# One fp32 decoder layer on one core: expert values by two-chunk dense products in place of gathered value rows

## What is computed

```
def chunk(xc):                                   # 128 tokens
    ...                                          # scores of two tables of 128 keys, for 8 heads
    best_s, best_j = lax.top_k(cand.reshape(C, Hh, K * K), K)
    expert = ia * PEER_KEYS + ib                 # 8 heads x 16 picks = 128 experts for each token
    g = jax.nn.softmax(best_s, axis=-1)
    u = u_tab[expert]
    a = jax.nn.gelu(jnp.einsum('cd,chkd->chk', xc, u))
    coeff = (g * a).astype(xc.dtype)
    return jnp.einsum('chk,chkd->cd', coeff, v_tab[expert])
```

## Time and profile before

| | |
|---|---|
| median of 3 runs | 3803.96 us (3799.67 to 3804.94) |
| span of the profiled execution, first to last instruction | 3789.9 us |
| what the median has beyond that span | 14.1 us |
| TensorE busy (weight loads) | 2933.6 us, 77% (1517.5 us, 40%) |
| VectorE busy | 2484.4 us, 66% |
| ScalarE busy | 1298.0 us, 34% |
| GpSimd busy | 1420.4 us, 37% |
| moved by DMA | 1297.10 MB, mean 342 GB/s |
| of it by gathers (queue q0) | 1073.83 MB, 72.2% of 16 engines' span |

### The profile page before, as it was taken

How to read it: one execution, slowest core, us unless ns; L and a number is a source line. 1 busy time by engine, 2 the same in 40 slices (tenths; PEclk the granted TensorE clock), 3 DMA queues, 4 the chain that set the end, 5 groups by cost and what they waited for, 6 DMA issues and landing times.

```text
span 3789.9 us, 34958 instructions
## 1 busy us (share of the span) xinstructions
PE 2933.6 (77%) x8920; PEld 1517.5 (40%) x8920; DVE 2484.4 (66%) x5699; ACT 1298.0 (34%) x3333; POOL 1420.4 (37%) x1367
## 2 busy tenths in 40 slices
PE   8797866984886598989689797787878777766665
PEld 6655533431443355555344343333333333322222
DVE  0321218786876477767437888877887887788765
ACT  1212312221121244444234544444443454344333
POOL 0000003443776376657423333333333333333332
PEclk9897888997898799999899999999989999999999
DMA  7844156777998999999889999999999999999998
GB/s 298 274 147 184 57 215 214 238 263 283 346 338 327 352 369 341 363 352 355 333 318 369 401 411 417 409 414 415 411 407 421 413 405 407 421 410 414 417 411 351
DMA packets 274454, 1297.10 MB, mean 342 GB/s; under 512 B 27888, under 2 KB 63088, under 8 KB 180464
## 3 DMA queue, kind: packets, MB, share of 16 engines
q0 software_dynamic: 195120, 1073.83, 72.2%
q1 hardware_dynamic: 74384, 203.74, 14.4%
q10 hardware_dynamic: 4752, 17.30, 1.2%
HBM read 1231.07 MB, written 63.70 MB: 342 GB/s over the span
## 4 chain that ended last, share of the span: by engine, by line
DMA 31%; issue 7%; DVE 5%; PE 4%; ACT 3%; POOL 0%; POOLq 0%; DVEq 0%; SPq 0%; ACTq 0%
DMA s_ring<-peer_uv,s_expert 17%; DMA e_more_slots<-peer_uv,s_expert 10%; PE e_acc L503 3%; DVE e_part L427 1%; PE e_product L1859 1%; DMA e_more_slots<-peer_v,s_expert 1%; DMA next_h<-e_h 1%; DMA e_h<-norm_ffn_row 1%; DMA s_scratch<-norm_final_row 1%; DVE s_ring L394 1%; ACT L341 1%; ACT s_diagonal L324 0%; ACT s_gate L343 0%; DVE s_dots L394 0%; DVE e_more_slots L394 0%
## 5 line engine op out<-in xcount | busy, mean ns | idle before, releaser
L503 PE MATMUL e_acc<-s_ring,s_diagonal 128*128 128x512 f32 (+1 forms) x2168 | 898.8, 543 | 379.6 <-ACT s_diagonal L324 352.8
L394 DVE CUSTOM_DVE_ANT_0 s_ring<-s_ring,e_x_copy 128x1024 f32<-128x1024 f32 x548 | 666.6, 1217 | 221.9 <-DMA s_ring<-peer_uv,s_expert 215.1
L503 PEld LDWEIGHTS e_acc<-s_ring,s_diagonal 128*128 128x128 f32 x2168 | 396.5, 199 | 943.5 <-ACT s_diagonal L324 587.5
L278 POOL DMA_INDIRECT s_ring<-peer_uv,s_expert x462 | 437.5, 947 | 783.1 <-DVE e_part L427 551.8
L278 POOL DMA_INDIRECT s_ring<-peer_u,s_expert x331 | 377.4, 1140 | 449.9 <-DVE s_expert L1796 230.8
L503 PE MATMUL e_acc<-e_more_slots,s_diagonal 128*128 128x512 f32 (+1 forms) x948 | 387.4, 536 | 153.9 <-ACT s_diagonal L324 146.3
L278 POOL DMA_INDIRECT s_ring<-peer_v,s_expert x325 | 373.2, 1148 | 332.0 <-PE e_acc L503 94.9
L341 ACT ACTIVATE s_dots<-s_dots 128x1 f32<-128x1 f32 x704 | 142.2, 202 | 961.3 <-DVE s_dots L394 959.0
L324 ACT ACTIVATE s_diagonal<-s_ident,s_gate 128x128 f32<-128x128 f32 x949 | 371.2, 399 | 223.0 <-PE e_acc L503 100.1
L278 POOL DMA_INDIRECT e_more_slots<-peer_uv,s_expert x231 | 217.6, 942 | 413.8 <-DVE e_part L427 273.5
L394 DVE CUSTOM_DVE_ANT_0 s_ring<-s_ring,s_x 128x1024 f32<-128x1024 f32 x245 | 299.5, 1222 | 104.6 <-DMA s_ring<-peer_u,s_expert 69.2
(11 more groups left out here) (233 smaller groups left out, 3618.5 us busy)
## 6 DMA issues: line engine op xcount, KB each, us to landing
w_in_kept<-w_in SPq DMA_DIRECT2D x8, 1104.0 KB, 11.8
w_in_gained<-w_in_kept SPq DMA_DIRECT2D x8, 1104.0 KB, 10.2
p_w_in<-w_in_gained SPq DMA_DIRECT2D x8, 1104.0 KB, 19.0
f_w_big<-w_mem_kv SPq DMA_DIRECT2D x4, 2048.0 KB, 19.2
f_w_big<-peer_w_q_t SPq DMA_DIRECT2D x2, 4096.0 KB, 17.9
peer_scores<-f_stage_s SPq DMA_DIRECT2D x16, 512.0 KB, 8.5
e_mem_scores<-mem_scores SPq DMA_DIRECT2D x2, 4096.0 KB, 14.6
e_mem_values<-mem_values SPq DMA_DIRECT2D x2, 4096.0 KB, 25.0
```

The source lines that it names most:

```text
L278: pool.indirect_dma_start(out=to, out_offset=None, in_=table, in_offset=bass.IndirectOffsetOnAxis(ap=self.expert[c % PICK_BUFFERS][:, k:k ...
L394: dve.tensor_tensor_reduce(row, row, x[:, :], 1.0, 0.0, ALU.mult, ALU.add, self.dots[:, k:k + 1]).then_inc(self.u_used, 1)
L503: last = pe.matmul(self.acc[:, at:to], self.diagonal[:, made % DIAGONALS, :], row[:, at:to], start=(n == group[0]), stop=(n == group[-1]))
```

## The change

V rows are not gathered any more. All picks come first; then a new last block, `sum_values`, works on pairs of chunks (256 tokens), in the order (6,7), (0,1), (2,3), (4,5). For each pair:

- **Spread.** For each token, its 128 picks become two matrices of 128 picks by 128 places: `one_a` has a one at the pick's `a`, `one_b` the coefficient at its `b`. Their product on TensorE is the token's coefficient for each of the 16384 experts. VectorE builds them for four tokens at a time (`hot_batch`), ScalarE copies the product out of PSUM into `d_coeffs` (16384 experts by 256 tokens).
- **Sum.** For each of the 128 values of `b`, a tile of V with 128 experts by 1024 (0.5 MB, a plain DMA by SP, 4 buffers) is multiplied with the coefficients of both chunks: four matmuls of 512 columns, accumulated over all 128 tiles.
- **Dense pair.** Chunks 6 and 7 gather nothing, and get their dot products with all of U: for each `b` a tile of U, transposed in HBM, times the transposed `x` of 256 tokens (8 matmuls of 256 columns), a Gelu by ScalarE and a product with `d_coeffs` by VectorE.

Chunks 0 to 5 still gather their U rows: 768 positions, one each, through a ring of 6 slots. The Gelu and the gate of a chunk are applied at once. Blocks 2 and 3 now take four chunks, blocks 4 to 6 the other four. The list stands at position 105, 225, 430 and 548 where blocks 3, 4, 5 and 6 end, and the other 220 rows are read beside `sum_values` (`BESIDE`: 16, 8 and 8 of them beside the spreads of the first three pairs).

```
-PAIRS_FROM = 331
-STAGES = [(PICK_FIRST, "pe", D), (PROJECT_REST, "split", 0), (ATTEND_REST, "split", BANK), (len(ROWS), "pe", 3 * D // 4)]
-FIRST = 3
-PICK_FIRST, PROJECT_REST, ATTEND_REST = 150, 300, 640
+RING = 6
+PAIR = 2
+VALUE_GROUPS = (((6, 7), True), ((0, 1), False), ((2, 3), False), ((4, 5), False))
+GATHERED = CHUNKS - PAIR
+ROWS = GATHERED * PICKS
+FIRST = 4
+PICK_FIRST, PROJECT_REST, ATTEND_REST, PICK_REST = 105, 225, 430, 548
...
+            def hot_batch(batch, i):
+                n, q = divmod(i, P // BATCH)
+                at = BATCH * (batch % (HOT // BATCH))
+                need(dve, spread_done, batch - HOT // BATCH + 1)
+                a, b, coeff = (picked[:, n, k, BATCH * q:BATCH * (q + 1)] for k in range(3))
+                dve.tensor_tensor(one_a[:, at:at + BATCH, :], lanes[:, :].unsqueeze(1).to_broadcast([P, BATCH, P]),
+                                  a.unsqueeze(2).to_broadcast([P, BATCH, P]), ALU.is_equal).then_inc(hot_ready, 1)
+                for t in range(BATCH):
+                    dve.tensor_scalar(one_b[:, at + t, :], lanes[:, :], b[:, t:t + 1], coeff[:, t:t + 1], ALU.is_equal,
+                                      ALU.mult).then_inc(hot_ready, 1)
...
+                    act.activation(coeffs[:, i // (P // BATCH), :, at:at + BATCH],
+                                   spread_to[batch % SPREAD][:, :].rearrange("p (t b) -> p b t", t=BATCH),
+                                   ACT.Copy).then_inc(spread_kept, 1)
...
+                        last = pe.matmul(spread_to[batch % SPREAD][:, P * t:P * (t + 1)], one_a[:, at + t, :], one_b[:, at + t, :],
+                                         start=True, stop=True)
...
+                for b in range(PEER_KEYS):
+                    if dense and b + 2 < PEER_KEYS:
+                        dot(g, b + 2)
+                    tile = wait_tile("v", g, b)
+                    if dense:
+                        pe.wait_ge(coeffs_ready, b + 1)
+                    for i in range(PAIR):
+                        for half in range(2):
+                            at = slice(BANK * half, BANK * (half + 1))
+                            last = pe.matmul(acc[i][:, at], coeffs[:, i, b, :], tile[:, at], start=(b == 0), stop=(b == PEER_KEYS - 1))
+                    last.then_inc(tile_used, 1)
```

More of the change, by code:

```diff
@@ L40 @@
 PICKS = PEER_HEADS * TOPK
-RING = 8
 GROUP_STEPS = 4 * 5 + 2 + 2 * 5 + 3 + 6 + 2
@@ L116, with __init__ @@
+GATHERED = CHUNKS - PAIR
+ROWS = GATHERED * PICKS
+GELU_AFTER, COEFF_AFTER = 3, 6
+STREAM_END = ROWS + COEFF_AFTER + 1
 class Stream:
-    def __init__(self, nc, io, sb, sb_early, sem, stages):
+    def __init__(self, nc, io, sb, sem):
         self.nc, self.io = nc, io
-        self.stages = [(start, until, mode) for start, (until, mode, _) in zip([0] + [u for u, _, _ in stages], stages)]
-        self.columns = [columns for _, _, columns in stages]
-        assert all(mode == "split" or columns == D or s == len(stages) - 1 for s, (_, mode, columns) in enumerate(stages))
@@ L141, in __init__ @@
-        self.ring = sb("s_ring", [P, RING, D])
[L142 to L148, removed]
+        self.expert = sb("s_expert", [P, CHUNKS, PICKS], U32)
+        self.gate = sb("s_gate", [P, CHUNKS, PICKS])
+        self.dots = sb("s_dots", [P, 2, PICKS])
+        self.x = sb("s_x", [P, 2, D])
+        self.ring = sb("s_ring", [P, RING, D])
@@ L158, in __init__ @@
+        self.activated, self.coeff_ready = sem("s_activated"), sem("s_coeff_ready")
         self.passed_pool = sem("s_passed_pool")
         self.eps_set, self.ident_loaded = sem("s_eps_set"), sem("s_ident_loaded")
[L161 to L180, removed]
-            self.pe_through.append(pe)
-            self.dve_through.append(dve)
-            if n == wide_from:
-                free = list(range(RING, WIDE_RING)) + free
-            slot = free.pop(0)
-            free.append(slot)
-            self.slot.append(slot)
-            self.before.append(last_in.get(slot))
-            last_in[slot] = n
@@ L223, in summed @@
-    def summed(self, c):
-        return sum(1 + (self.mode(CHUNK_END[d]) == "pe" and self.pe_columns(CHUNK_END[d]) < D) for d in range(c + 1))
-    def row(self, n):
-        slot = self.slot[n]
-        return self.ring[:, slot, :] if slot < RING else self.more_slots[:, slot - RING, :]
-    def wait_row(self, eng, n):
-        first = n - 1 if n >= PAIRS_AT and ROWS[n][0] == "v" else n
-        eng.wait_ge(self.row_loaded[self.slot[first]], 16 * self.loads[first])
-    def group(self, c, s):
-        start, until, _ = self.stages[s]
-        return [V_AT[g] for g in range(PICKS * c, PICKS * (c + 1)) if start <= V_AT[g] < until]
@@ L1566, in pick_chunks @@
         gain_kept = chunks[0] == 0
-        b.gain = stream.scratch if gain_kept else b.h
-        stream.acc = ps("e_acc", [P, D])
-        stream.x_copy = ps("e_x_copy", [P, D])
-        if last and stream.columns[-1] < D:
-            stream.part = sb("e_part", [P, D - stream.columns[-1]])
+        b.gain = sb("e_gain", [P, D]) if gain_kept else b.h
         block = ctx.enter_context(nc.Block())
```

652 lines of the change are left out of this document (304 added, 348 removed).

## The result

The changed kernel takes 5121.85 us (median of 4 runs, 5116.54 to 5127.27) against 3804.45 us for the kernel before (4 runs, 3799.67 to 3807.48). The ratio is 1.3477, its 95% interval 1.3435 to 1.3519. The forecast was 5020 us with a range of 4850 to 5300.

What follows compares the result with a forecast made beforehand. The prediction took block 6, 1924 of 3790 us, to be paced by DMA gathers. Blocks 1 to 6 at 2355 us plus the new block at 2652 gave 5007, plus 14 around the span: 5020 us, range 4850 to 5300.

Steps and rivals of the forecast that it cites:

- Price of a matmul, sums and dots: New last block: fp32 matmuls at 0.859 us for 512 columns, 0.432 for 256; sums 1759 us, dots 442 us.
- Spread: New last block: 256 batches at 1.35 us, VectorE the last of three engines; 346 us.
- Seams and rows: New last block: 36 us for rows beside the spreads, 69 us for start, pair ends, handovers and end.
- Blocks before: Blocks 1 to 6, with four chunks and fewer gathers, end at 2355 us.
- Block 5: Attention over 26 of 30 key blocks with 205 U rows, TensorE and VectorE equally full; 430 us, bounds 355 to 545.
- Cheaper products: Rival: new matmuls run as one record, a quarter of the price; kernel 3379 us; chance 0.01.
- The pace of handovers: Rival: handovers between engines set the spread's pace, 2.5 us a batch; kernel 5315 us; chance 0.13.
- The blocks before gain nothing: Rival: blocks 5, 3 and 6 cost 545, 600 and 586 us despite fewer gathers; kernel 5235 us; chance 0.12.
- They gain more: Rival: block 5 at 360 us and picks at 80 us a chunk; kernel 4894 us; chance 0.11.

Runs made afterwards that it cites:

- e4_v_bf16: Changed kernel with the coefficients and each tile of V rounded to bf16 before the sum, 8 tile buffers instead of 4; 4037.87 us.
- e3_no_one_a: Changed kernel with the wide one-hot product one_a left out in all batches of the spread but the first two; 4968.77 us.
- e1_fill: Changed kernel with two idle 512-column matmuls ahead of each of block 5's 64 units, and a wait for w_out before the first score; 5108.56 us.
- e5_fill_one: Changed kernel with one idle 512-column matmul ahead of each of block 5's 64 units, on keys there from the start; 5074.66 us.
- e2_rows_out: Changed kernel with 160 of block 5's 205 U rows moved beside the sums; 4981.48 us.
- e9_pool_two: Changed kernel, in fp32, with two of VectorE's four narrow products of a spread batch given to GpSimd; 5226.22 us.
- e7_u_bf16: As e4_v_bf16, with the tiles of U and x for the dots of chunks 6 and 7 also rounded to bf16; 3936.05 us.
- e8_hot_bf16_fill: As e7_u_bf16, with the spread's one-hot products in bf16 and one idle matmul for each unit of block 5; 3914.57 us.

## Why the prediction was right, and where it was not

- **Price of a matmul, sums and dots** (1759 + 442 us): right, 2203 us measured. The three dense stretches of the kernel before gave the price, and e4_v_bf16 shows that it is the price of fp32 operands. The prediction had it right because it read the number of records beside the number of matmuls.
- **Spread** (346 us): the mechanism was right (VectorE last of the three, shown by e3_no_one_a), the size low. The step that failed is the scalar form, taken as 0.185 us between neighbours of 32 and 1024 columns; four take 1.63 - 0.61 = 1.02 us, 0.255 each. That is 256 x 0.28 = 72 us more, inside the bounds named.
- **Seams and rows** (36 + 69 = 105 us): 2697 - 2203 - 417 = 77 us, 28 less. The block came to 2697 us against 2652.
- **Blocks before.** End of block 2: 600 against 588; block 3: 518 against 550; block 4: 246 against 251; block 6: 529 against 536.
- **Block 5** (430 us, bounds 355 to 545): 525 us. This is the term that was mis-sized most. Its step was TensorE at (541 - 188) x 26 / 30 = 306 us, taken from the old clock of 0.93. The work was right, 312 us in e1_fill at 0.97; the time was 450 us at 0.67. That the removed L503 products had kept TensorE at its 2.4 GHz level is what the idle matmuls in their place speak for (e1_fill, e5_fill_one); no run puts L503 itself back. The second part is VectorE's rows in front of the attention's steps (e2_rows_out, 144 us for 160 rows), most of which passes through the same clock.
- **Rivals.** Cheaper products are out by the records. The pace of handovers is out by e3_no_one_a. "The blocks before gain nothing" came true for one block of three: block 5 came near its 545, blocks 3 and 6 stayed far below its 600 and 586. "They gain more" came true for block 3 alone (518 us, 522 at its 80 us a chunk).

Sum of the deviations: 12 - 32 - 5 + 95 - 7 + 45 = 108 us in the span, 5007 forecast and 5115 measured. Around the span the forecast had 14 us, and the median lies 7 us above it (5121.85 against 5114.8), so that the time is 102 us above the forecast of 5020, and block 5 alone is 95 of them. Inside the new block 72 us too little for the spread and 28 us too much for seams and rows partly cancel, which is luck. The sign and the size of the loss can be told in one sentence: 336 MB fewer bytes are worth 0.82 ms at 410 GB/s, and 2.2 ms of fp32 products and 0.4 ms of one-hot batches stand in series behind the picks.

## What to carry to other kernels

Before trading transfers for matmuls, count the matmuls in the type that they run in: a matmul of 512 columns took 0.859 us in fp32 and 0.22 in bf16, and here the type of the sums alone makes the difference between 5122 and 4038 us. When work is taken away from TensorE, ask what its clock will be afterwards; the price of the work that stays is the price at that clock. A stretch that one engine fills while the others stand still (the spread) can be moved beside another stretch: that took 150 us off the last block (1537 to 1387 us), while bf16 outputs took 5 us off it and GpSimd's help made it longer.

## What the runs showed that I had not expected

- Adding 55 or 110 us of idle matmuls to block 5 made its attention 52 us shorter than in the changed kernel (some 40 us over all runs). The granted clock went from 0.67 to 0.87 and 0.97.
- Across runs whose block 5 is the same instruction for instruction, its length moves with the clock: 511 us at 0.65 (e9_pool_two), 504.5 at 0.67, 498 at 0.70 (e3_no_one_a), 482 and 473.5 at 0.72 (e4_v_bf16, e7_u_bf16). What sets which of these a kernel gets, no run shows.
- GpSimd takes 1.01 us for a product of 128 columns with VectorE at work beside it, and VectorE takes 0.255. The only wider product that GpSimd has here, 1024 columns of another operation (a multiplication, L1079), takes 1.11 us, hardly more. How much of the 1.01 us is a fixed part is not shown, since the two forms differ in more than their length. The Trainium skill, page GPSIMD Engine Reference, names two software dispatch hops for a GpSimd instruction in its section Elementwise — side-by-side cycle accounting, which would fit a fixed part; no run here looks inside it.
- In the first spread of e8_hot_bf16_fill TensorE is busy for 67.88 us of 135 and its granted clock is 0.50, the 1.2 GHz level; the spread is no longer for that (136 us in the changed kernel), since VectorE is last.
